# An encoder layer's attention: the product with v in two matmuls instead of three, the denominator on VectorE, the remainders on GpSimd

## The chip, the cores and the metric

The kernel runs on one NeuronCore of a Trainium2 chip. The metric is the time on the device of one launch, in microseconds (us). The launch holds six stages that run one after the other on the same core.

## The reference

One transformer layer on 1024 prompt tokens and 2048 sample tokens, each group with 16 learned meta tokens in front of it. Eight heads of grouped-query attention (GQA, 64 wide, two key/value heads) and eight heads of latent attention (MLA, query and key 96 wide, value 64 wide), an output projection, a mixture of experts and a last norm:

```python
s = einsum('bqhgd,bkhd->bhgqk', q, k) * scale      # per head; q of the group against its keys
p = softmax(s, axis=-1)                            # over the group's keys and the 16 meta keys
o = einsum('bhgqk,bkhe->bqhge', p, v)
h += W_out[ norm(GQA(u)) | norm(MLA(u)) ],  u = RMSNorm(h)
h += HierMoE(RMSNorm(h));  out = RMSNorm(h)[:, 16:]
```

Everything is float32. The kernel multiplies in `float32r`, a rounded form; a factor that has to be exact is split into a rounded part (`hi`) and a remainder (`lo`), and the products of the parts are added up in PSUM.

## The kernel before, in words

**Stages.** `stage_project` makes q, k and v of all heads and stores their hi and lo parts in DRAM; `stage_attend` computes attention; then come the output projection, the routing, the experts and the last norm. The change touches the first two.

**Attention's items.** A head's work is a fixed list of 86 items. An item is 128 keys (a chunk) against 512 queries (a block). There are six blocks, four of the sample (16 chunks and the 16 meta keys: 17 items each) and two of the prompt (8 chunks and the meta keys: 9 items each); a block's meta item is its last. So a head has 80 full items and 6 meta items. Every engine walks the same list in its own program, with semaphores between them.

**One item.** TensorE (`qk`, line 1064) makes the scores transposed, keys by queries, in one of two banks `psS`: two matmuls for a GQA head, three for an MLA head. The row maximum has been put in as one more row of the product, so that ScalarE (`exp`, line 936) can read the bank twice with Exp, once into the rounded `p_hi` and once into the exact `prob`. VectorE (`remainder`, line 981) subtracts them into `p_lo`; for eight of the items GpSimd does so (line 929). Then TensorE (`pv`, line 1075) adds v_hi p_hi + v_lo p_hi + v_hi p_lo into a bank `psO`, three matmuls of 512 columns, two items behind `qk`. v has a column of ones as its 65th, so that the bank's 65th row is the denominator. `p_hi`, `p_lo` and `prob` have four slots. GpSimd makes v_hi and v_lo of the next head itself (`split`, line 897).

**The maxima of the next head.** In the same slots each engine also does a piece of the next head's row maxima: TensorE a matmul of 128 queries by 512 keys into one of two banks `psM` (`unit`, line 1098), VectorE a maximum over it (line 996). There are 80 such units, laid over 72 of the slots; 24 small matmuls into `psK` do the meta keys (line 1105). `finish` joins the maxima, `row` turns them and sends them through DRAM into a row of q.

**The end of a block.** ScalarE copies `psO` to `oT` (`o_out`), TensorE turns it with four transposes (`o_turn`, line 1117), VectorE multiplies by the reciprocal of the denominator (`normalise`, line 1015), and the result is stored.

**Projection.** For each pair of token tiles `mla` (line 626) makes eight units in two banks `psX`; the two `v` units are copied out by ScalarE alone (line 416), the `k` and `n` units by ScalarE and VectorE. A bank is free for the unit after next when its last reader has gone over it. GpSimd copies the GQA heads' v (line 330).

## Time and profile before

| | us |
|---|---|
| three runs: lowest, median, highest | 4121.14, 4127.71, 4137.02 |
| the profiled execution, its own time | 4129.44 |
| its span, first to last instruction | 4127.6 |
| granted TensorE clock, mean over the span | 0.952 of full speed |

Busy shares over the span are TensorE 91%, VectorE 67%, ScalarE 58%, GpSimd 13%. They are means over six stages with different limits, so they say little of one stage. "Busy" of a matmul counts from its start to a modelled end, and successive ones overlap; the same holds to a lesser degree of VectorE and ScalarE. What an instruction costs in a full queue is the distance from its start to the next one's start, here called its pitch.

### The profile page before, as it was taken

How to read it: one execution, taken by the hardware profiler on the slowest of the kernel's cores; microseconds unless marked ns; L12 is line 12 of the kernel's file. 1: busy time of each engine (PE TensorE's matmuls, PEld its weight loads, DVE VectorE, ACT ScalarE, POOL GpSimd, SP SyncE). 2: the span in 40 equal slices, each digit the busy share in tenths (PEclk: the TensorE clock that was granted, in tenths of full speed). 3: DMA queues.
4: the chain of work that ended last, by engine and by line, in shares of the span. 5: the costliest groups of instructions: out<-in, count | busy, mean ns of one | idle time of the engine just before them, and what ended most of it. 6: DMA issues, size and time to landing. Idle time of an engine off the chain costs nothing. (4 is left out here: it accounts for less than half of the span.)

```text
span 4127.6 us, 59990 instructions
## 1 busy us (share of the span) xinstructions
PE 3739.1 (91%) x16747; PEld 2729.3 (66%) x16748; DVE 2763.0 (67%) x4425; ACT 2377.5 (58%) x4123; POOL 554.9 (13%) x553
## 2 busy tenths in 40 slices
PE   7999948999999999999999999996999569999992
PEld 7888825666666666667667666764777456666661
DVE  5656547878878898878677777854343556666564
ACT  4443304777777777766676666676333135555554
POOL 0000000111111111110110111100000013333331
PEclk9999967999999999999999999998999889999996
DMA  4464570220222112221121122002333158888787
GB/s 164 153 218 160 189 187 16 61 54 20 56 62 61 44 33 52 61 61 26 41 60 42 25 61 49 16 7 90 137 129 135 53 169 240 239 244 251 230 239 270
DMA packets 308135, 454.66 MB, mean 110 GB/s; under 512 B 118230, under 2 KB 245490, under 8 KB 296850
## 3 DMA queue, kind: packets, MB, share of 16 engines
q1 hardware_dynamic: 241942, 359.85, 29.1%
q0 software_dynamic: 18576, 67.64, 6.9%
q10 hardware_dynamic: 47376, 24.26, 2.0%
q8 instruction: 115, 1.88, 0.2%
q14 instruction: 126, 1.03, 0.1%
HBM read 305.68 MB, written 146.05 MB: 109 GB/s over the span
## 5 line engine op out<-in xcount | busy, mean ns | idle before, releaser
L940 ACT ACTIVATE b_p_hi<-b_psS 128x512 fp32r<-128x512 f32 (+1 forms) x1376 | 822.0, 597 | 587.6 <-PE b_psS L1071 575.8
L1071 PE MATMUL b_psS<-b_q,b_k 96*128 96x512 f32 (+3 forms) x3440 | 1051.3, 403 | 24.7 <-issue 18.2
L988 DVE TENSOR_TENSOR b_p_lo<-b_prob,b_p_hi 128x512 fp32r<-128x512 f32 x1152 | 830.1, 722 | 252.3 <-ACT b_prob L943 207.1
L943 ACT ACTIVATE b_prob<-b_psS 128x512 f32<-128x512 f32 (+1 forms) x1376 | 815.0, 592 | 1.1
L1071 PEld LDWEIGHTS b_psS<-b_q,b_k 96*128 96x128 f32 (+3 forms) x3440 | 628.0, 186 | 255.9 <-issue 25.6
L996 DVE TENSOR_REDUCE b_mx_s<-b_psM 128x1 f32<-128x512 f32 x1024 | 691.5, 687 | 86.6 <-PE b_psM L1102 66.6
L1102 PE MATMUL b_psM<-b_k,b_q 128*128 128x512 f32 (+1 forms) x1280 | 516.1, 424 | 54.2 <-DMA b_v<-V 39.4
L1094 PE MATMUL b_psO<-b_p_hi,b_v_hi 128*65 128x512 f32 x1280 | 516.2, 403 | 26.3 <-DVE b_p_lo L988 24.4
L1094 PE MATMUL b_psO<-b_p_hi,b_v_lo 128*65 128x512 f32 x1280 | 509.5, 398 | 0.0
L1094 PE MATMUL b_psO<-b_p_lo,b_v_hi 128*65 128x512 f32 x1280 | 509.0, 398 | 0.0
L929 POOL TENSOR_TENSOR b_p_lo<-b_prob,b_p_hi 128x512 fp32r<-128x512 f32 x128 | 166.6, 1301 | 1684.8 <-ACT b_prob L943 1684.8
L1102 PEld LDWEIGHTS b_psM<-b_k,b_q 128*128 128x128 f32 (+1 forms) x1280 | 251.7, 197 | 157.5 <-DVE b_mx_s L996 52.4
L1094 PEld LDWEIGHTS b_psO<-b_p_lo,b_v_hi 128*65 128x65 f32 x1280 | 175.9, 137 | 125.3 <-issue 5.1
L1094 PEld LDWEIGHTS b_psO<-b_p_hi,b_v_hi 128*65 128x65 f32 x1280 | 176.6, 138 | 118.9 <-DVE b_p_lo L988 51.3
L1094 PEld LDWEIGHTS b_psO<-b_p_hi,b_v_lo 128*65 128x65 f32 x1280 | 177.2, 138 | 110.1 <-issue 4.0
L2051 PE MATMUL e_psG<-e_w_gu,e_xT 128*128 x512 | 233.2, 598 | 11.0 <-SPq L1874 10.0
L612 PE MATMUL a_psZ<-a_w_hi,a_xT_hi 128*128 128x396 f32 x600 | 209.4, 349 | 24.6 <-DVE a_w_lo L569 24.6
L612 PE MATMUL a_psZ<-a_w_hi,a_xT_lo 128*128 128x396 f32 x600 | 207.3, 345 | 0.0
L612 PE MATMUL a_psZ<-a_w_lo,a_xT_hi 128*128 128x396 f32 x600 | 206.5, 344 | 0.0
L996 DVE TENSOR_REDUCE b_mx_p<-b_psM 128x1 f32<-128x512 f32 x256 | 173.9, 687 | 30.7 <-PE b_psM L1102 27.6
L1934 ACT ACTIVATE e_wg_hi<-e_w_gu 128x2048 fp32r x64 | 122.7, 1917 | 106.5 <-SPq L1874 85.2
L2000 DVE TENSOR_TENSOR e_wd_lo<-e_w_dn,e_wd_hi 128x2048 fp32r<-128x2048 f32 x64 | 146.7, 2292 | 37.6 <-ACT e_wd_hi L1948 35.8
(247 smaller groups left out, 5274.9 us busy)
## 6 DMA issues: line engine op xcount, KB each, us to landing
e_w_gu<-w_gate SPq DMA_DIRECT2D x32, 1024.0 KB, 7.7
e_w_gu<-w_up SPq DMA_DIRECT2D x32, 1024.0 KB, 10.0
e_w_dn<-w_down SPq DMA_DIRECT2D x32, 1024.0 KB, 13.6
a_x_raw<-xallT SPq DMA_DIRECT2D x25, 512.0 KB, 5.0
a_x<-xall SPq DMA_DIRECT2D x25, 512.0 KB, 4.2
c_o<-O SPq DMA_DIRECT2D x24, 512.0 KB, 4.8
c_x<-xall SPq DMA_DIRECT2D x24, 512.0 KB, 3.6
H<-c_h SPq DMA_DIRECT2D x24, 512.0 KB, 2.7
```

What stands on the lines that cost most here:

```text
L612: i = nc.tensor.matmul(psZ[:, b, 0:ZW], xx[:, s, c, :], ww[:, c, b * ZW:b * ZW + ZW], start=n == 0, stop=n == 3 * KC - 1)
L929: nc.gpsimd.tensor_tensor(p_lo[:, slot, :], prob[0:kn, slot, :], p_hi[0:kn, slot, :].bitcast(F32), ALU.subtract).then_inc(lo_ready_pool, 1)
L940: nc.scalar.activation(p_hi[0:kn, (s * NI + j) % NP, :], psS[0:kn, j % 2, :], ACT.Exp)
L943: nc.scalar.activation(prob[0:kn, (s * NI + j) % NP, :], psS[0:kn, j % 2, :], ACT.Exp).then_inc(p_ready, 1)
L988: nc.vector.tensor_tensor(out, prob[0:kn, slot, :], p_hi[0:kn, slot, :].bitcast(F32), ALU.subtract).then_inc(lo_ready, 1)
L996: nc.vector.tensor_reduce(dst, psM[:, u % 2, :], AX.X, ALU.max).then_inc(m_free, 1)
L1071: m = nc.tensor.matmul(psS[0:kn, j % 2, :], kk[s][0:r, k], qq[s][0:r, q], start=n == 0, stop=n == len(passes) - 1)
L1094: m = nc.tensor.matmul(psO[0:VC, b % 2, :], vv[s][:, vc, :], pp[:, slot, :], start=first and n == 0, stop=last and n == 2)
L1102: nc.tensor.matmul(psM[:, u % 2, :], q0[s][0:r, q * P:q * P + P], k0[s][0:r, kc:kc + 512], start=True, stop=True).then_inc(m_psum, 1)
L1934: nc.scalar.activation(wg_hi[:, :, :], w_gu[:, bass.ds(w * KC, HK), :], ACT.Copy).then_inc(wg_rounded, 1)
L2000: nc.vector.tensor_tensor(wd_lo[:, c, :], w_dn[:, bass.ds(w * HC, HC), :], wd_hi[:, c, :].bitcast(F32), ALU.subtract).then_inc(wd_ready, 1)
L2051: nc.tensor.matmul(psG[:, s, :], xT[:, c - HK, :], w_gu[:, bass.ds(w * KC + c, 1), :].rearrange("p o n -> p (o n)"), start=c == HK, stop=F ...
```

## The change

**v side by side.** v's hi and lo parts are made in the projection stage and stored next to each other, 128 columns for each head (`VC = 2 * VD`), and loaded as one stationary tile. One matmul with `p_hi` and one with `p_lo` (`pv_hi`, `pv_lo`) then give hi and lo sums in the two halves of `psO`'s 128 rows. The column of ones is gone. The two halves are added at the end of the block: for GQA heads by a matmul with a doubled identity (`pair_id`) in place of the transpose, for MLA heads by transposes back into `psO` and an add on VectorE.

**The denominator.** VectorE adds every `prob` tile to an accumulator in a PSUM bank, `acc`, three items late (`den_add`), the last one of a block into `accS` in SBUF. `o_turn` sums it over the partitions: a one-column matmul for GQA, a transpose and a VectorE sum for MLA.

**The remainders.** GpSimd makes `p_lo` of all 80 full items. VectorE makes the remainder of meta items only.

**Meta keys.** They are the second item of each block rather than the last, and are stored both ahead of and behind the other keys. The maxima's units take them in: five units of 412 or 414 columns for a sample tile and three of 346 or 348 for a prompt tile, 104 units over 68 slots. The 24 small matmuls go.

**Depths.** Six slots instead of four; `pv_hi` two items behind `qk`, `pv_lo` four; `o_out`, `o_turn`, `normalise` and the store one or two items later.

```diff
-VC = VD + 1
+VC = 2 * VD
@@ projection, GpSimd v_copy
                 for copy in range(2):
-                    i = nc.gpsimd.tensor_copy(vst_g[:, b, j, copy:PAIRS:2, 0:VD],
-                                              z[:, s, ZV:ZCQ].rearrange("p (h c) -> p h c", c=VD))
+                    nc.gpsimd.tensor_copy(vst_g[:, b, j, copy:PAIRS:2, 0:VD].bitcast(F32R), src)
+                pool.drain()
+                for copy in range(2):
+                    i = nc.gpsimd.tensor_tensor(vst_g[:, b, j, copy:PAIRS:2, VD:VC].bitcast(F32R), src,
+                                                vst_g[:, b, j, copy:PAIRS:2, 0:VD], ALU.subtract)
@@ projection, VectorE mla_out
-                    if kind == "k":
+                    if kind == "v":
+                        r = META if B is None else P
+                        i = nc.vector.tensor_tensor(vst_m[0:r, j, :, VD:VC].bitcast(F32R),
+                                                    psX[0:r, u % 2, :].rearrange("p (h c) -> p h c", c=VD),
+                                                    vst_m[0:r, j, :, 0:VD], ALU.subtract)
+                    elif kind == "k":
@@ attention, items and units
-        R = 4
-        SPAN = 72
+        R = 6
+        HI_LAG, LO_LAG, DEN_LAG = 2, 4, 3
+        SPAN = 68
@@ attention, GpSimd
+                slot = slot_of(s, j)
+                pool.wait_ge(p_ready, h * NI + j + 3)
+                nc.gpsimd.tensor_tensor(p_lo[:, slot, :], prob[:, slot, :], p_hi[:, slot, :].bitcast(F32),
+                                        ALU.subtract).then_inc(lo_ready, 1)
@@ attention, ScalarE exp
-                act.wait_ge(pv_done, h * NI + j + 1)
+                act.wait_ge(pv_done, h * NI + j + 1 + NP - reuse(s, j))
+                act.wait_ge(den_done, h * NI + j + 1 + NP - reuse(s, j))
@@ attention, VectorE
+            def den_add(h, s, j):
+                _, _, kn, _, first, last = ITEMS[j]
+                slot = slot_of(s, j)
+                dve.wait_ge(p_ready, h * NI + j + 3)
+                if kn == META:
+                    nc.vector.tensor_tensor(p_hi[M_LO, slot, :], prob[0:kn, slot, :], p_hi[0:kn, slot, :].bitcast(F32),
+                                            ALU.subtract).then_inc(meta_lo_ready, 1)
+                dve.wait_ge(den_done, h * NI + j + NP)
+                if first:
+                    m = nc.vector.tensor_copy(acc[:, :], prob[:, slot, :])
+                else:
+                    out = accS[:, BLOCK_OF[j] % 2, :] if last else acc[0:kn, :]
+                    m = nc.vector.tensor_tensor(out, acc[0:kn, :], prob[0:kn, slot, :], ALU.add)
+                m.then_inc(den_done, 1)
@@ normalise, MLA heads
+                nc.vector.tensor_reduce(den[:, :], psT[:, :].rearrange("p (j c) -> p j c", c=P), AX.X, ALU.add)
+                dve.drain()
+                nc.vector.reciprocal(rden[:, :], den[:, :])
+                dve.drain().then_inc(t_free, 1)
+                dve.wait_ge(o_stored[b % 2], stored)
+                nc.vector.tensor_tensor(o_lo[:, :, :], tv[:, :, VD:2 * VD], rr, ALU.mult)
+                nc.vector.tensor_tensor(ost[:, b % 2, :, :], tv[:, :, 0:VD], rr, ALU.mult)
+                dve.drain()
+                nc.vector.tensor_tensor(ost[:, b % 2, :, :], ost[:, b % 2, :, :], o_lo[:, :, :], ALU.add).then_inc(o_ready, 1)
@@ attention, TensorE
-                for n, (vv, pp) in enumerate(((v_hi, p_hi), (v_lo, p_hi), (v_hi, p_lo))):
-                    m = nc.tensor.matmul(psO[0:VC, b % 2, :], vv[s][:, vc, :], pp[:, slot, :],
-                                         start=first and n == 0, stop=last and n == 2)
+                nc.tensor.matmul(psO[:, b % 2, :], v[s][:, vc, :], p_hi[:, slot_of(s, j), :], start=first, stop=False)
...
+                pe.wait_ge(lo_ready, h * (NI - NB) + j - metas + 1)
+                nc.tensor.matmul(psO[:, b % 2, :], v[s][:, vc, :], p_lo[:, slot_of(s, j), :],
+                                 start=False, stop=last).then_inc(pv_done, 1)
@@ o_turn
+                    if gqa:
+                        nc.tensor.matmul(psT[:, c * VD:c * VD + VD], oT[:, b % 2, cc], pair_id[:, :], start=True, stop=True)
+                        m = nc.tensor.matmul(psT[:, SUP * VD + c:SUP * VD + c + 1], accS[:, b % 2, cc], ones[:, :],
+                                             start=True, stop=True)
+                        continue
+                    nc.tensor.transpose(psO[:, b % 2, cc], oT[:, b % 2, cc], ident[:, :])
+                    m = nc.tensor.transpose(psT[:, cc], accS[:, b % 2, cc], ident[:, :])
```

## Rows read from the trace of the kernel before

**Rows 1.** Page, first part: TensorE's busy time of the whole span.
```profile
PE 3739.1 (91%) x16747; PEld 2729.3 (66%) x16748; DVE 2763.0 (67%) x4425; ACT 2377.5 (58%) x4123; POOL 554.9 (13%) x553
```

**Rows 2.** Windows view: length, engines' busy us, clock; ahead of attention, and attention.
```profile
0.00:664.00 664.00, 553.56 (x2672) 481.07 (x2673) 377.21 (x937) 221.31 (x390) 27.82 (x69) 0.90 0.54 167
664.00:2838.00 2174.00, 2118.16 (x9331) 1460.43 (x9331) 1701.85 (x2715) 1582.03 (x2943) 267.86 (x226) 0.98 0.20 43
```

**Rows 3.** Windows view over seven GQA heads, then over six MLA heads.
```profile
777.31:1680.80 903.49, 871.82 (x3831) 589.28 (x3830) 753.04 (x1226) 690.44 (x1288) 124.25 (x105) 0.98 0.23 50
1821.19:2700.50 879.31, 860.76 (x3798) 606.18 (x3797) 674.65 (x1051) 596.40 (x1104) 105.34 (x90) 0.98 0.19 41
```

**Rows 4.** Timeline, VectorE: joining of the maxima, once a head; start, duration.
```profile
777.31 0.18 DVE L1006 TENSOR_TENSOR b_nmx<-b_nmx,b_nmx_m 128x24 f32<-128x24 f32 x1
...
1680.80 0.18 DVE L1006 TENSOR_TENSOR b_nmx<-b_nmx,b_nmx_m 128x24 f32<-128x24 f32 x1
```

**Rows 5.** Page, groups: busy us, mean ns of one | idle before, its releaser.
```profile
L996 DVE TENSOR_REDUCE b_mx_s<-b_psM 128x1 f32<-128x512 f32 x1024 | 691.5, 687 | 86.6 <-PE b_psM L1102 66.6
```

**Rows 6.** Timeline, TensorE, inside an MLA item: start, duration.
```profile
2300.69 0.39 PE L1102 MATMUL b_psM<-b_k,b_q 96*128 96x512 f32 x1
2300.91 0.39 PE L1094 MATMUL b_psO<-b_p_hi,b_v_hi 128*65 128x512 f32 x1
2301.14 0.39 PE L1094 MATMUL b_psO<-b_p_hi,b_v_lo 128*65 128x512 f32 x1
```

**Rows 7.** Timeline, TensorE: the 24 small matmuls of a head.
```profile
773.70 2.74 PE L1108 MATMUL b_psK<-b_k,b_q 128*128 128x16 f32 x24
```

**Rows 8.** Timeline, VectorE with a full queue.
```profile
827.82 0.68 DVE L988 TENSOR_TENSOR b_p_lo<-b_prob,b_p_hi 128x512 fp32r<-128x512 f32 x1
828.42 1.28 DVE L996 TENSOR_REDUCE b_mx_s<-b_psM 128x1 f32<-128x512 f32 x2
```

**Rows 9.** Tile view: the maximum over 384 columns; min/median/max ns.
```profile
L1001 DVE TENSOR_REDUCE b_nmx_m<-b_psK x16: 557/558/558, 655.1 to 2699.7; 128x24 f32<-128x384 f32 x16
```

**Rows 10.** Timeline, VectorE: a block's normalisation.
```profile
696.40 1.29 DVE L996 TENSOR_REDUCE b_mx_s<-b_psM 128x1 f32<-128x512 f32 x2
697.87 0.18 DVE L1019 RECIPROCAL b_rden<-b_psT 128x4 f32<-128x4 f32 x1 [0.18 <-issue]
698.23 0.42 DVE L1022 TENSOR_TENSOR b_ost<-b_psT,b_rden 128x256 f32<-128x256 f32 x1 [0.18 <-issue]
698.88 0.69 DVE L988 TENSOR_TENSOR b_p_lo<-b_prob,b_p_hi 128x512 fp32r<-128x512 f32 x1 [0.22 <-ACT b_prob L943]
```

**Rows 11.** Timeline: GpSimd and VectorE at the same time, VectorE reading SBUF twice.
```profile
786.54 2.46 POOL L916 TENSOR_TENSOR b_v_lo<-b_v,b_v_hi 128x1040 fp32r<-128x1040 f32 x1
...
786.64 3.51 DVE L988 TENSOR_TENSOR b_p_lo<-b_prob,b_p_hi 128x512 fp32r<-128x512 f32 x2 [0.21 <-issue]
```

**Rows 12.** The same with one of VectorE's inputs in PSUM.
```profile
746.75 1.30 POOL L929 TENSOR_TENSOR b_p_lo<-b_prob,b_p_hi 128x512 fp32r<-128x512 f32 x1 [10.11 <-ACT b_prob L943]
...
747.02 0.42 DVE L1022 TENSOR_TENSOR b_ost<-b_psT,b_rden 128x256 f32<-128x256 f32 x1 [0.16 <-issue]
```

**Rows 13.** Tile views: GpSimd's remainder, and a subtraction out of PSUM.
```profile
L929 POOL TENSOR_TENSOR b_p_lo<-b_prob,b_p_hi x128: 1270/1291/1567, 700.4 to 2827.4; 128x512 fp32r<-128x512 f32 x128
...
L541 DVE TENSOR_TENSOR a_stage<-a_psX,a_stage x26: 191/691/693, 70.4 to 540.7; 128x512 fp32r<-128x512 f32 x24, 128x32 fp32r<-128x32 f32 x2
```

**Rows 14.** Timeline, projection: the v units of one batch on TensorE and ScalarE.
```profile
181.72 1.88 PE L644 MATMUL a_psX<-a_w_vup,a_ckvT 128*128 128x512 f32 x4
184.86 1.99 PE L651 MATMUL a_psX<-a_ckvT,a_w_kup 128*128 128x256 f32 x8 [1.26 <-ACT a_vst_m L416]
...
184.23 1.06 ACT L416 ACTIVATE a_vst_m<-a_psX 128x512 f32<-128x512 f32 x2
```

**Rows 15.** Timeline, TensorE: maxima of the first head, before attention starts.
```profile
604.49 1.41 PE L1102 MATMUL b_psM<-b_k,b_q 128*128 128x512 f32 x2 [0.17 <-DVE b_mx_s L996]
606.07 1.41 PE L1102 MATMUL b_psM<-b_k,b_q 128*128 128x512 f32 x2 [0.17 <-DVE b_mx_s L996]
```

359 lines of the change are left out of this document (172 added, 187 removed).

## The prediction

> **What bounds the kernel now.** I read the page's first part, then the windows by stage, then single heads, then timelines for the pitch of each kind of instruction. TensorE leads on the page [rows 1]; attention is 2174 of the 4127.6 us [rows 2]. The joining of the maxima comes once a head, so the distance between two of them is a head's time [rows 4]. The same marks frame the windows [rows 3]: seven GQA heads take 903.49 us, 129.1 each; six MLA heads take 879.31, 146.5 each. TensorE is idle for 32 and 19 us there, so both kinds go by TensorE, MLA heads nearly without a gap. Its matmuls of 512 columns start 0.23 us apart [rows 6], although each lasts 0.39 there. VectorE is busy for 107.6 us of a GQA head's 129.1, ScalarE for 98.6: whatever goes onto VectorE has little room.
>
> **TensorE after.** A full item loses one matmul of three with v: 80 a head, 80 x 0.23 = 18.4 us. The stationary tile grows from 65 to 128 columns at no cost, since `qk` has 128 and keeps the 0.23 pitch [rows 6]. The 24 small matmuls go, 2.7 us [rows 7]. The units stay at nearly the same columns in shorter pieces: 80 x 0.188 + 24 x 0.16 = 18.9 us (412 and 346 columns at full clock, 0.172 and 0.144, and the 0.016 by which 0.23 exceeds 512 columns), against 80 x 0.23 = 18.4. The turns grow. For a 128-column stationary tile the nearest pitch is 2.74/24 = 0.11 us [rows 7]. MLA has eight a block, 0.9 us; GQA four matmuls with `pair_id` and four with `ones`, in float32, each listed as two instructions as L644 is (four rows for two units [rows 14]): 16 x 0.11 = 1.8 us. Sum for MLA: 86 x 3 + 80 x 2 + 6 = 424 matmuls x 0.23 = 97.5, units 18.9, turns 5.4: 122 us. GQA: 338 x 0.23 = 77.7, units 18.9, turns 10.7: 107 us.
>
> **VectorE after.** A 512-element instruction has a pitch of 0.60 us in a full queue, whether a subtraction or a maximum [rows 8]. Maxima: 687 ns at 512 columns [rows 5], 558 at 384 [rows 9], so 1.0 ns an element; 412 columns pitch at 0.50, 346 at 0.43, and the head's 104 take 40 + 10.4 = 50.4 us (80 x 0.60 = 48 before). Adds: 86 x 0.60 = 51.6, where 78 subtractions stood. Whether an add that also writes PSUM costs the same no row shows. From below it can't be under 0.60, the rate of any 512 elements; from above, a dependent instruction after a drain starts 0.18 after the end of the one before [rows 10], 0.69 + 0.18 = 0.87. I take 0.60: a subtraction that reads PSUM lasts 691 ns [rows 13], the SBUF one 0.68 or 0.69 [rows 8], and a maximum usually stands between two adds, which hides the wait on `den_done`. The Trainium skill ("VectorE: DVE Perf Modes", section "The TRN2 errata") gives a PSUM source 62 cycles more than an SBUF source; by it the 86 adds would cost 5.6 us a head more, 90 us in all. The trace disagrees: 691 ns out of PSUM against 0.68 to 0.69 us out of SBUF is no difference.
>
> A block's normalisation puts about 1.2 us between two other instructions [rows 10], from 696.40 + 2 x 0.60 to 698.88. GQA keeps it. MLA adds a 512-element sum (0.6), one more multiply and an add of 256 (0.35 each) and two drains (0.2 each): 2.9 us.
>
> **GpSimd after.** It takes 80 remainders of 1.29 us [rows 13]. What separates two in a row no row shows; between the shortest, 1.27, and the longest, 1.57, I take 1.3, which is 104 us a head. `split` goes. Beside it VectorE: a subtraction with both inputs in SBUF stood still until GpSimd's was over, 3.51 us for two [rows 11]. With one input in PSUM it kept its 0.42 us inside GpSimd's 1.30 [rows 12]. `den_add` reads PSUM and SBUF, so I cost no collision for it. The Trainium skill ("SBUF — State Buffer", section "SBUF: two separate sides") has this as an exclusive lock that a VectorE instruction takes if it has two SBUF inputs or runs in a two-port mode; by that rule, the trace agrees. Two-SBUF instructions are left: the meta remainder, and the MLA heads' last add. Each waits for a running 1.29, half of it on average, 0.65 us. The stall behind L916, 3.51 - 0.60 - 0.69 = 2.2 us a head, goes.
>
> **A head.** In the 68 slots with units GQA has on VectorE: adds 40.8, maxima 50.4, four meta remainders 2.4 and their waits 2.6, three normalisations 3.6: 99.8 us, against TensorE's 88 (268 matmuls, the units, four turns) and 64 x 1.3 = 83 of GpSimd. VectorE ends last. In the other 18 slots GpSimd does, 16 x 1.3 = 20.8 (ScalarE's 98.6/86 is at most 1.15 an item). Together 120.6; I add 2.9 for the clock, granted at 0.98 [rows 3], and for trading places: 123.5. MLA, VectorE: 40.8 + 50.4 + 2.4 + 2.6 + 3 x 2.9 + 3 x 0.65 = 106.9, TensorE 100. Other slots: 18 adds one after another at 0.75, 13.5, meta 1.2, three normalisations 8.7, the joining and row 1.5: 24.9. Together 131.8, with 4.2 for bursts of VectorE that hold up a TensorE only 7 us ahead: 136.
>
> **Elsewhere.** Projection: a v bank is now freed by VectorE after ScalarE, 0.69 later [rows 13], and TensorE already waits 1.26 there [rows 14]; 12 batches x 0.8 = 10 us. At the other end it may be nothing, if TensorE makes it up; twice that if VectorE comes late. GpSimd's two more small subtractions a tile hide in a tile's time, some 20 us (L541's first to last, 470 us, for 24 tiles [rows 13]). V grows from 65 to 128 columns a head. Mid-stage that hides; at the change of stages the last store (256 tokens x 8 heads x 63 x 4 bytes, 0.5 MB) and the first head's sample load (0.5 MB) take 3 us each at 167 GB/s [rows 2] if nothing covers them; I take 4 (0 to 8). The first head's maxima run ahead of everything at 1.58 us for two [rows 15]; 100 columns fewer save 0.10 on each engine at 1.0 ns a column, 166 fewer 0.17, so two take 1.39 and 1.25, and all 104 take 70.6 us instead of 63.2, less 0.6 for L1001: +7. Eight extra stores of meta columns, once, hide in SP's queue.
>
> **Sum** against the execution's own 4129.4 us: GQA 8 x (129.1 - 123.5) = 45; MLA 8 x (146.5 - 136) = 84; costs 10 + 4 + 7 = 21. 4129.4 - 45 - 84 + 21 = 4021. The median of the runs is 1.7 lower: **4020 us**, 2.6% faster. The 80 x 16 matmuls alone are worth 294 us; over half is lost to VectorE.
>
> **Rivals.**
> TensorE stays the bound: the added depth evens VectorE out, and nobody meets the lock. GQA 118 (VectorE's sum without waits), MLA 122 plus 3 for the clock, 125: 8 x 11.1 + 8 x 21.5 - 21 = 240, 3890 us. For it: six slots. Against it: `psM` still has two banks, so TensorE can run at most two units ahead.
> GpSimd becomes the bound: remainders at 1.57 us, the longest seen [rows 13], 80 of them 126 us. GQA 130, MLA 138: 4129 + 7 - 68 + 21 = 4090 us. For it: meta and add instructions hold the lock against it too. Against it: the median is 1.29.
> Slower than before: the accumulator in PSUM serialises VectorE. Every add costs 0.87 instead of 0.60, 86 x 0.27 = 23 us more in heads in which VectorE ends last. 4021 + 16 x 23 = 4389 us. With a price of only 0.065 it would be 4021 + 89 = 4110, no change. It passes the time before once an add costs 109/(16 x 86) = 0.08 us more than I took. For it: each add waits on the one before, and no row shows such a write. Against it: [rows 12, 13].
> The change does not do its part only if the two matmuls pitched like three; `qk` rules that out.
>
> **How the numbers follow.** My forecast 0.53 (3970 to 4070), TensorE 0.20, GpSimd 0.13, the add at 4110 0.03, at 4389 0.11. A measurement of this kernel tells no change from a difference of 0.5%, 21 us. Faster by more: 0.53 + 0.20 + 0.10 of GpSimd's case = 0.83; within: its other 0.03 and the add's 0.03, 0.06; slower: 0.11. The range reaches from just above TensorE's case over GpSimd's to the add at 4110: 3900 to 4120. It leaves out the dear add and the lower end of TensorE's case, some 0.2.
>
> **What would show it.** The joinings 121 to 126 us apart in GQA heads and 133 to 140 in MLA heads; VectorE's idle time small in both; `den_add` at 0.69 us listed and 0.60 pitch beside GpSimd instructions of 1.29; TensorE waiting on VectorE at `psM`; k units of the projection waiting 2 us. A `den_add` above 0.75, or GpSimd above 1.4, would make the forecast wrong upwards; GQA heads under 118, downwards.

## The result, and the profile after

Four runs of the changed kernel took 4303.23 to 4317.05 us, median 4312.33; four of the kernel before 4121.14 to 4137.02, median 4125.83. The ratio is 1.0439, with a 95% interval from 1.0416 to 1.0461. The forecast was 4020 us, 2.6% faster; the kernel became 4.4% slower, and the time lies outside the range.

The windows view (length, busy us of TensorE, its weight loads, VectorE, ScalarE, GpSimd, granted clock, DMA share, GB/s) of the changed kernel, by stage, answers to [rows 2]:

```profile
0.00:684.00 684.00, 556.69 (x2675) 483.04 (x2677) 402.05 (x987) 222.17 (x391) 39.85 (x105) 0.89 0.57 178
684.00:3018.00 2334.00, 2135.84 (x8818) 1624.00 (x8816) 1916.70 (x3414) 1519.88 (x2844) 1659.71 (x1280) 0.91 0.20 45
3018.00:4309.80 1291.80, 1067.73 (x4744) 786.98 (x4744) 682.73 (x771) 574.18 (x792) 249.21 (x258) 0.93 0.62 193
```

The windows are cut at round times. By the trace's own marks, the first Exp of attention and the next stage's first load, attention starts 19 us later (21 were forecast) and takes 155 us more, where it was to become 129 us shorter. The stages behind it, which the change does not touch, take 1295 us (1287 before; 1287 to 1299 in the experiments below). The same view over seven GQA heads and six MLA heads, between the same marks as [rows 3]:

```profile
803.60:1813.03 1009.43, 936.78 (x3779) 690.29 (x3779) 817.82 (x1479) 663.13 (x1246) 727.37 (x560) 0.89 0.23 51
1957.88:2876.19 918.31, 822.36 (x3464) 646.20 (x3463) 765.17 (x1375) 573.26 (x1068) 622.62 (x481) 0.93 0.21 47
```

A GQA head takes 144.2 us instead of 129.1, an MLA head 153.1 instead of 146.5. TensorE has fewer matmuls, yet is busy longer in GQA heads (936.78 against 871.82): the granted clock fell from 0.98 to 0.89, and in MLA heads to 0.93. The clock knows two levels, 2.4 and 1.2 GHz, so 0.89 means that 32.1 us of each GQA head ran at half clock (5.4 before), and 0.93 means 22.2 us of each MLA head (5.9 before).

The sizes of single instructions are those forecast. From the page's groups (busy us, mean ns of one | idle before, releasers) and the listing of VectorE's meta remainder in GQA heads (min/median/max ns):

```profile
L931 POOL TENSOR_TENSOR b_p_lo<-b_prob,b_p_hi 128x512 fp32r<-128x512 f32 x1280 | 1660.8, 1311 | 833.1 <-ACT b_prob L951 817.4
L1002 DVE TENSOR_TENSOR b_acc<-b_acc,b_prob 128x512 f32<-128x512 f32 (+1 forms) x1184 | 817.1, 690 | 64.1 <-issue 37.9
L1010 DVE TENSOR_REDUCE b_mx_s<-b_psM 128x1 f32<-128x412 f32 (+1 forms) x1280 | 706.1, 578 | 180.1 <-PE b_psM L1130 168.1
...
L995 DVE TENSOR_TENSOR b_p_hi<-b_prob,b_p_hi x42: 681/1534/1825, 813.9 to 1807.8; 16x512 fp32r<-16x512 f32 x42
```

An add in PSUM lasts 690 ns and has the pitch of 0.60 us. The meta remainder, 0.68 us by itself, lasts 1.53 in the median and 1.39 in the mean: it waits for a running GpSimd instruction, 0.71 us on average instead of the 0.65 forecast.

What was not forecast is what happens where VectorE's work comes in one piece. VectorE and then TensorE at the end of a GQA block (start, duration; in brackets idle time before, and what ended it):

```profile
739.75 0.57 DVE L1010 TENSOR_REDUCE b_mx_s<-b_psM 128x1 f32<-128x412 f32 x1
740.36 1.52 DVE L995 TENSOR_TENSOR b_p_hi<-b_prob,b_p_hi 16x512 fp32r<-16x512 f32 x1
741.81 0.68 DVE L1002 TENSOR_TENSOR b_acc<-b_acc,b_prob 16x512 f32<-16x512 f32 x1
742.52 1.08 DVE L1010 TENSOR_REDUCE b_mx_s<-b_psM 128x1 f32<-128x412 f32 x2
...
740.91 0.64 PE L1099 MATMUL b_psS<-b_q,b_k 128*128 128x512 f32 x2
743.16 0.46 PE L1130 MATMUL b_psM<-b_k,b_q 128*128 128x414 f32 x1 [1.61 <-DVE b_mx_s L1010]
743.46 0.40 PE L1111 MATMUL b_psO<-b_p_hi,b_v 128*128 128x512 f32 x1
743.79 0.49 PE L1118 MATMUL b_psO<-b_p_hi,b_v_meta 48*128 48x512 f32 x1
744.21 0.52 PE L1145 MATMUL b_psT<-b_pair_id,b_oT 128*128 128x64 f32 x2
744.52 0.53 PE L1146 MATMUL b_psT<-b_ones,b_accS 128*128 128x1 f32 x2
```

For 2.2 us VectorE reads no bank of `psM`. TensorE has filled both and stands still for 1.61 us. At 744.4, 1.3 us behind the stop and just as the block's turn with its 64- and 1-column matmuls has begun, the clock falls to half. The windows view of the next 6.8 us, and TensorE in them:

```profile
744.50:751.30 6.80, 6.80 (x26) 6.19 (x26) 2.58 (x6) 1.28 (x3) 1.27 (x1) 0.50 0.00 0
...
748.48 0.55 PE L1130 MATMUL b_psM<-b_k,b_q 128*128 128x412 f32 x1
748.82 0.63 PE L1111 MATMUL b_psO<-b_p_hi,b_v 128*128 128x512 f32 x1
749.25 0.55 PE L1130 MATMUL b_psM<-b_k,b_q 128*128 128x412 f32 x1
```

512 columns now take 0.43 us and not 0.23, TensorE is busy all the time, and VectorE only 2.58 of 6.80 us: for that long TensorE is the bound. In MLA heads the piece is the normalisation:

```profile
2356.19 1.08 DVE L1010 TENSOR_REDUCE b_mx_s<-b_psM 128x1 f32<-128x412 f32 x2 [0.92 <-PE b_psM L1130]
2357.44 0.69 DVE L1039 TENSOR_REDUCE b_den<-b_psT 128x4 f32<-128x512 f32 x1 [0.17 <-issue]
...
2359.33 0.90 DVE L1047 TENSOR_TENSOR b_ost<-b_ost,b_o_lo 128x256 f32<-128x256 f32 x1
...
2361.38 0.46 PE L1130 MATMUL b_psM<-b_k,b_q 96*128 96x414 f32 x1 [2.35 <-DVE b_mx_s L1010]
```

A third place is the start of a head. The row of maxima goes to DRAM and back by the sync engine's queue. Its issues around one MLA head's start, then TensorE's first matmul of that head:

```profile
1953.44 0.51 SPq L857 DMA_DIRECT2D b_q<-QNH  x1
...
1958.45 0.40 SPq L857 DMA_DIRECT2D b_v<-V  x1
1963.54 7.84 SPq L891 DMA_DIRECT2D MX<-b_nmxT  x1
1975.07 0.23 SPq L894 DMA_DIRECT2D b_q<-MX  x1
...
1977.22 1.64 PE L1099 MATMUL b_psS<-b_q,b_k 97*128 97x512 f32 x3 [4.28 <-DMA b_q<-MX]
```

The store comes 5 us behind nine large loads and its issue takes 7.84 us (4.5 in the median of the 16 heads); before the change it came 13 us behind them and took 0.3. TensorE's waits by releaser (total us, times, longest), in the six MLA heads of the kernel before and then of the changed one:

```profile
PE b_psO L1094 <- DVE b_p_lo L988: 8.7, 6, 1.5
PE b_psS L1071 <- issue: 6.6, 2, 3.5
PE b_psM L1102 <- DVE b_mx_s L996: 3.3, 2, 2.1
```

```profile
PE b_psM L1130 <- DVE b_mx_s L1010: 43.5, 36, 2.4
PE b_psS L1099 <- DMA b_q<-MX: 26.8, 6, 5.8
PE b_psM L1130 <- DVE b_mx_p L1010: 15.2, 12, 2.3
```

### The profile page after: what moved, and what is told of

The parts are those of the page before. It is cut to its first block and busy times, and to the rows that moved or that the text cites. A ratio compares the mean times of both kernels' runs of the same rounds, so it can differ in the third digit from the quotient of the medians.

```text
span 4309.8 us, 62526 instructions
## 1 busy us (share of the span) xinstructions
PE 3760.3 (87%) x16235; PEld 2894.0 (67%) x16236; DVE 3001.5 (70%) x5171; ACT 2316.2 (54%) x4027; POOL 1948.8 (45%) x1642
## 5 line engine op out<-in xcount | busy, mean ns | idle before, releaser
L931 POOL TENSOR_TENSOR b_p_lo<-b_prob,b_p_hi 128x512 fp32r<-128x512 f32 x1280 | 1660.8, 1311 | 833.1 <-ACT b_prob L951 817.4
L1002 DVE TENSOR_TENSOR b_acc<-b_acc,b_prob 128x512 f32<-128x512 f32 (+1 forms) x1184 | 817.1, 690 | 64.1 <-issue 37.9
L1010 DVE TENSOR_REDUCE b_mx_s<-b_psM 128x1 f32<-128x412 f32 (+1 forms) x1280 | 706.1, 578 | 180.1 <-PE b_psM L1130 168.1
L1130 PE MATMUL b_psM<-b_k,b_q 128*128 128x412 f32 (+7 forms) x1664 | 669.9, 409 | 184.7 <-DVE b_mx_s L1010 102.9
L1111 PE MATMUL b_psO<-b_p_hi,b_v 128*128 128x512 f32 x1280 | 537.6, 420 | 0.2 <-ACT b_prob L951 0.2
L1123 PE MATMUL b_psO<-b_p_lo,b_v 128*128 128x512 f32 x1280 | 531.9, 416 | 0.7 <-POOL b_p_lo L931 0.7
L1111 PEld LDWEIGHTS b_psO<-b_p_hi,b_v 128*128 128x128 f32 x1280 | 261.6, 204 | 57.0 <-issue 2.2
L1123 PEld LDWEIGHTS b_psO<-b_p_lo,b_v 128*128 128x128 f32 x1280 | 260.3, 203 | 35.9 <-POOL b_p_lo L931 1.2
L1010 DVE TENSOR_REDUCE b_mx_p<-b_psM 128x1 f32<-128x346 f32 (+1 forms) x384 | 185.7, 510 | 20.0 <-PE b_psM L1130 19.1
L2088 PEld LDWEIGHTS e_psG<-e_w_gu,e_xT 128*128 128x128 f32 x512 | 98.1, 192 | 118.0 <-issue 113.3
```

The costliest lines, as they stand in the source:

```text
L931: nc.gpsimd.tensor_tensor(p_lo[:, slot, :], prob[:, slot, :], p_hi[:, slot, :].bitcast(F32), ALU.subtract).then_inc(lo_ready, 1)
L1002: m = nc.vector.tensor_tensor(out, acc[0:kn, :], prob[0:kn, slot, :], ALU.add)
L1010: nc.vector.tensor_reduce(dst, psM[:, u % 2, 0:n_keys], AX.X, ALU.max).then_inc(m_free, 1)
L1111: nc.tensor.matmul(psO[:, b % 2, :], v[s][:, vc, :], p_hi[:, slot_of(s, j), :], start=first, stop=False)
L1123: nc.tensor.matmul(psO[:, b % 2, :], v[s][:, vc, :], p_lo[:, slot_of(s, j), :], start=False, stop=last).then_inc(pv_done, 1)
L1130: nc.tensor.matmul(psM[:, u % 2, 0:kn], q0[s][0:r, q * P:q * P + P], k0[s][0:r, kc:kc + kn], start=True, stop=True).then_inc(m_psum, 1)
```

## The experiments

Theory A: TensorE stops where VectorE's work comes in one piece at a block's end and where the row is late, and the clock falls behind such stops; stops and half clock together are the loss. Theory B: VectorE's sum is the bound, the clock costs nothing. Theory C: the clock falls because TensorE has less to do throughout. "Half" is the time at half clock, "stops" TensorE's idle stretches above 0.6 us, both in us per head, from each profiled execution.

A fall is a drop of the granted clock from full to half. In the changed kernel's six MLA heads all 26 falls began inside a stop or within 1.7 us behind one. In its seven GQA heads 7 of the 33 falls began behind a stop and ahead of the turn, 5 at a turn with no stop before it, and 21 when a stop and the first matmuls of the turn both lay in the 3.1 us before, so that there the two causes cannot be told apart. Over the windows of all 18 profiled executions of the table (stops that began at half clock, 61, left out), none of the 204 stops of 0.6 to 1.5 us was followed by a fall within 4 us, 254 of the 309 of 1.5 to 2.5 us were, and 188 of the 191 longer ones; MLA heads by themselves give 0 of 133, 150 of 200 and 92 of 93.

The kernel before was run again beside each group of experiments, with medians 8 us apart, so small differences between groups are better read from the ratios. x1, x3 and x4 rest on two runs each.

| kernel | median us | ratio to before (95%) | GQA head, half, stops | MLA head, half, stops |
|---|---|---|---|---|
| before | 4126 to 4134 | 1 | 129.1, 5.4, 3.5 | 146.5, 5.8, 3.1 |
| after | 4312.33 | 1.0439 (1.0416 to 1.0461) | 144.2, 32.1, 8.9 | 153.1, 22.2, 15.2 |
| x1_fill | 4432.74 | 1.0737 (1.0687 to 1.0787) | 146.3, 14.1, 5.7 | 168.3, 21.0, 13.4 |
| x2_noden | 4133.62 | 1.0008 (0.9993 to 1.0024) | 127.7, 13.7, 6.0 | 146.1, 15.9, 12.8 |
| x3_metapool | 4220.29 | 1.0222 (1.0173 to 1.0271) | 134.9, 17.1, 7.7 | 150.7, 20.5, 15.5 |
| x4_spread | 4203.59 | 1.0182 (1.0136 to 1.0228) | 135.5, 18.0, 5.4 | 147.3, 15.9, 13.1 |
| x5_row | 4353.42 | 1.0537 (1.0519 to 1.0554) | 150.6, 41.3, 13.8 | 150.3, 17.6, 15.5 |
| x6_all3 | 4167.04 | 1.0090 (1.0073 to 1.0106) | 133.9, 16.6, 8.6 | 143.3, 13.7, 12.5 |
| x7_all3_turnfill | 4197.69 | 1.0167 (1.0148 to 1.0185) | 138.2, 10.7, 6.1 | 143.2, 13.1, 12.3 |
| x8_all3_split | 4155.99 | 1.0070 (1.0049 to 1.0092) | 133.8, 16.1, 8.6 | 142.3, 14.8, 11.5 |
| x9_rowact | 4276.54 | 1.0344 (1.0319 to 1.0369) | 144.5, 35.2, 8.7 | 147.9, 17.1, 11.7 |
| x10_best | 4103.56 | 0.9926 (0.9901 to 0.9952) | 129.7, 10.2, 4.0 | 139.2, 7.4, 8.9 |
| x11_best_late | 4167.26 | 1.0074 (1.0047 to 1.0100) | 132.5, 10.7, 6.0 | 145.6, 14.8, 12.5 |
| x12_best_pair | 4106.98 | 0.9924 (0.9894 to 0.9953) | 130.0, 10.7, 4.5 | 138.8, 12.5, 1.6 |
| x13_inter | 4096.92 | 0.9921 (0.9902 to 0.9940) | 128.2, 7.3, 3.8 | 139.6, 9.1, 8.6 |
| x14_inter_pair | 4072.17 | 0.9860 (0.9840 to 0.9879) | 128.4, 6.8, 4.2 | 135.4, 5.1, 1.5 |
| x15_late8 | 4117.54 | 0.9970 (0.9958 to 0.9982) | 132.5, 12.7, 4.3 | 139.6, 9.7, 8.4 |
| x16_early | 4103.26 | 0.9939 (0.9925 to 0.9952) | 130.4, 10.7, 5.5 | 138.9, 9.1, 3.7 |

**x1_fill.** Each matmul of the maxima is issued twice.

```diff
+                nc.tensor.matmul(psM[:, u % 2, 0:kn], q0[s][0:r, q * P:q * P + P], k0[s][0:r, kc:kc + kn],
+                                 start=True, stop=True)
                 nc.tensor.matmul(psM[:, u % 2, 0:kn], ...
                                  start=True, stop=True).then_inc(m_psum, 1)
```

> Every maxima matmul of the changed kernel is issued twice into the same bank, which changes no result: 104 x 0.16 to 0.19 = 19 us more TensorE work a head, evenly spread. Theory A (TensorE stops at block ends because VectorE's work comes in one piece there, and these stops take the clock to half): the stops stay, the extra work delays VectorE little; time 4300 to 4400, clock in attention up by 0.01 to 0.03 from 0.91. Theory B (VectorE's sum is the bound and the clock costs nothing): within 1% of 4312. Theory C (the clock falls because TensorE's stream is thinner all along): clock back to 0.97, time 4200 to 4260.

Half clock in GQA heads went from 32.1 to 14.1 us and stops from 8.9 to 5.7, but the head took 2.1 us more. The 104 extra matmuls cost 18.9 us by the forecast's own price; 9 of it is the half clock's gain, and most of the rest went into time in which TensorE had waited. So the clock does matter (B alone falls), but this filler did not pay for itself, and the time is above what each theory gave. That more work brought the clock back in GQA heads is also what C says. In MLA heads, where TensorE had little slack, the filler cost 15.2 and the half clock stayed, since the stops did; by C it should have gone.

**x2_noden.** All but the first copy and the last add of a block are left out.

```diff
+                if not first and not last:
+                    dve.sem_inc(den_done, 1)
+                    return
```

> Of the denominator's adds only the first copy and the last add of a block are made; the rest is left out, so outputs are wrong by the denominator. VectorE loses 74 adds of 0.60 us a head, 44 us. Theory A: stops mostly go, clock back to 0.96 or more, GQA heads near 118 us, MLA near 130, time about 4129 - 8 x 11 - 8 x 16 + 21 = 3935. Theory B: the same time, by VectorE's sum alone, 3900 to 3950, clock no matter. Theory C: TensorE's stream is as thin as in the changed kernel, so the clock stays near 0.91 and the time stays above 4050.

179 us less, so much of the loss hangs on VectorE's load, but 4134 is 200 above A and B. VectorE is busy for 72.1 us of a GQA head's 127.7 here: it can't be the bound by its sum. C's time fits (above 4050), but not its clock, which is 0.95 in both windows and not 0.91. 12.8 us of stops are left in an MLA head, at the two places that do not depend on the adds:

```profile
PE b_psM L1133 <- DVE b_mx_s L1013: 30.2, 18, 1.8
PE b_psS L1102 <- DMA b_q<-MX: 28.9, 6, 5.8
```

**x3_metapool.** GpSimd makes the meta item's remainder too, so that no VectorE instruction of a GQA head waits for GpSimd's hold on SBUF.

```diff
+                if ITEMS[j][2] == META:
+                    pool.wait_ge(lo_ready, h * (NI - NB) + j - BLOCK_OF[j])
+                    nc.gpsimd.tensor_tensor(p_hi[M_LO, slot, :], prob[0:META, slot, :], p_hi[0:META, slot, :].bitcast(F32),
+                                            ALU.subtract).then_inc(meta_lo_ready, 1)
+                    return
...
-                if kn == META:
-                    nc.vector.tensor_tensor(p_hi[M_LO, slot, :], prob[0:kn, slot, :], ...
```

> The meta remainder is made by GpSimd, so VectorE has no instruction with two SBUF inputs left in GQA heads. Theory A: the 0.6 us and the 0.8 us wait for GpSimd's lock go from every block end, stops shrink from 1.65 to under 0.5 us in GQA heads, the clock there recovers to 0.94 or more, GQA heads 144 to 132, MLA 153 to 150; time about 4190. Theory B: 6 x 1.4 = 8 us a head less in GQA, 4 in MLA, 4215. Theory C: as B for the stop, clock unchanged, 4250 to 4280.

92 us less for 96 instructions moved, whose whole time on VectorE was 116 us with their waits. The gain is mostly in GQA heads, 9.3 us each (2.4 in MLA heads); half of the half clock went. By its time alone, 4220, this is B's forecast (4215) rather than A's (4190); the clock in GQA heads, 0.94, is what A said. The stops at `psM` became shorter but did not fall under 0.5 us: 11 of 1.0 to 1.5 us stood there, and no fall of the clock followed one of them. With `psM` out of the way TensorE now waited for the late row in GQA heads too, 25.9 us in seven, against 1.8 in the changed kernel.

**x4_spread.** The same 104 units, but none in the seventh slot behind a block's last item, where VectorE normalises, and about half as many in the two before it.

```diff
+        SHARE = [0.0 if j - 7 in END_OF else 0.55 if j - 5 in END_OF or j - 6 in END_OF else 1.0
+                 for j in range(R, R + SPAN)]
         for u in range(NU):
-            UNIT_AT.setdefault(R + u * SPAN // NU, []).append(u)
+            at, k = (u + 0.5) / NU * sum(SHARE), 0
+            while sum(SHARE[:k + 1]) <= at:
+                k += 1
+            UNIT_AT.setdefault(R + k, []).append(u)
```

> The same 104 maxima units, but one instead of one or two in the slots five and six behind a block's end and none in the seventh, where VectorE normalises. No work is added or removed. Theory A: the stops at psM shrink, the clock recovers by 0.02 to 0.04, time 4200 to 4260. Theory B: the same sum on VectorE, 4300 to 4320. Theory C: no change of clock, within 0.5% of 4312.

No engine has less to do, and the time falls by 109 us, 8.7 us per GQA head and 5.8 per MLA head. Half clock in GQA heads fell from 32.1 to 18.0 us with TensorE's work unchanged, where C forecast no change. This is the plainest proof that no engine's sum set the time.

**x5_row.** The sync engine sends the maxima's row ahead of the next sample load.

```diff
+                row(h + 1, 1 - s, nxt)
                 if more:
                     sp.wait_ge(pv_done, h * NI + SAMPLE_LAST + 1 + NP)
                     load(h + 2, i + 1, s, kind, "s")
-                row(h + 1, 1 - s, nxt)
```

> The sync engine issues the next head's maxima row (store to DRAM, load back) ahead of the sample load of the head after, nothing else changed. Theory A (part of it): the row came late because its store was queued right behind 8 to 10 large sample loads (issue of store to issue of load 6 to 13 us after, 2 to 4.6 before). Then the stop at a head's start goes: 4.4 to 5.8 us for each of 7 MLA starts, 2 to 3 for each GQA start, with the half-clock stretch behind it (MLA 22 us of half clock a head to about 15), 4312 - 7 x 5 - 8 x 2.5 - 7 x 3 = about 4235. Theory C (the stop at a head's start is hidden time, VectorE's sum decides): within 10 us of 4312. Rival: the large loads are then late in turn and the time stays; the stop would move from the row to the load.

41 us slower, where A gave 77 less: the rival. The wait on the row went, and this came in its place, with half clock behind it (MLA heads):

```profile
PE b_psM L1130 <- DMA b_v<-V: 36.6, 6, 9.8
```

**x6_all3** is x3, x4 and x5 in one.

> Three edits in one: the meta item's remainder on GpSimd (alone -92 us), fewer maxima units in the two slots behind a block's end and none in the third (alone -109), the row ahead of the sample load. If each removes a stop of its own, the gains add: 4312 - 92 - 109 - 60 = about 4050, half clock under 10 us per GQA head. If the first two remove the same stop (the lump of VectorE's work at a block's end), the result is 4312 - 110 - 60 = about 4140 and half clock stays at 15 to 18 us per GQA head. I expect between them, 4100.

4167, and again a wait for v's load of up to 8.6 us, 5.3 us a head (36.5 and 32.1 us in the two windows). 4100 was expected. The three edits' own differences, -92, -109 and +41, would give 4152: x3 and x4 nearly add up, x5's edit is the wrong mend.

**x7_all3_turnfill.** As x6, with a wide matmul behind each of three pairs of a GQA turn.

```diff
+                        if c < SUP - 1:
+                            nc.tensor.matmul(psT[:, 260:512], ident[:, :], oT[:, b % 2, 0:252], start=True, stop=True)
```

> As the kernel with three edits, with one more matmul of 252 columns (exact float32, its output unused) behind each of the first three pairs of a GQA turn. It tests what takes the clock to half right behind a GQA turn. If it is the turn's narrow matmuls (64 columns and 1 column), the dips that begin 0 to 1.5 us behind a GQA turn (some 18 of 23 in seven heads) go and half clock falls below 5 us per GQA head; the fillers themselves cost 18 x 0.42 = 7.6 us per GQA head, so the time is about equal to slightly above the kernel without them. If it is a stop that precedes, the dips stay and the time is 50 to 60 us above. MLA heads: no change.

In x6 nine of twelve falls of the clock in seven GQA heads began 0.2 to 1.7 us behind the end of a turn, with no stop before it; here none of seven did, and all seven stand at long stops. Half clock fell from 16.6 to 10.7 us, not below 5 as expected, and the time rose by 31, as the fillers cost. MLA heads are unchanged. So a stretch of 1- and 64-column matmuls can take the clock down with no stop, though it does not always: 9 of x6's 42 turns had a fall behind them.

**x8_all3_split.** As x6; the last multiply and add of an MLA normalisation come one slot later.

```diff
+                    if j - 8 in END_OF:
+                        normalise_2(h, END_OF[j - 8], gqa)
```

> As the kernel with three edits, with the second half of an MLA head's normalisation (one multiply, one add, 0.9 + 0.4 us) moved one slot later. Theory A: the stop of 1.7 to 2.3 us at an MLA block's end comes from VectorE's work in one piece; cut in two, with psM's two banks between, it falls by 1.0 to 1.3 us, six times a head: 147 to about 141 per MLA head, 8 x 6 = 48 us less. If VectorE's sum decides, nothing (within 10 us). GQA heads: no change.

1.0 us per MLA head, not 6; the two medians differ by 11 us and their ranges overlap. That VectorE's wait for the turn, in the half that was not moved, makes the stop instead is what x11 and x15 try.

**x9_rowact.** The changed kernel, the row's two DMAs on ScalarE's queue three and six slots behind its making.

```diff
+                    if not last and j == ROW_AT + 3:
+                        row_store(act, h + 1)
+                    if not last and j == ROW_AT + 6:
+                        row_load(act, h + 1, 1 - s, nxt)
```

> The next head's maxima row goes through DRAM by two DMAs of ScalarE's queue, three and six slots behind the row's making, instead of the sync engine's queue behind the sample load; that load stays where it was. Theory A: the stop at a head's start (MLA 4.4 to 5.8 us, GQA 2 to 3) goes and, unlike with the row issued ahead of the load on the sync engine, no load comes late in its place: 4312 - 6 x 5 - 8 x 2.5 - the half clock behind them (some 6 us less at half clock per head, each worth 0.5 us, 14 x 3 = 42) = about 4220. Rival: the stop is only hidden time of VectorE's sum, within 15 us of 4312.

5.1 us less per MLA head, nothing in GQA heads: 36 us, where 92 were expected. In the changed kernel the late row was a cost of MLA heads alone; its GQA heads had waited for it for only 1.8 us in seven, so there was no stop to remove.

**x10_best** is x3, x4 and x9 in one.

> Meta remainder on GpSimd, units kept away from the slots behind a block's end, and the row by ScalarE's queue. The kernel with the row ahead of the load on the sync engine took 4167 and showed a wait of 6 us a head for v's load (half of it is the row's move). Without that wait 6 us for each of 14 heads go and half clock falls to some 10 us per head: 4167 - 14 x 6 + 0 = about 4085 (range 4060 to 4120), faster than before (4129). If VectorE's sum (123 us busy per GQA head, 137 per MLA head) is the bound now, it stays at 4140 or above.

4103.56, within the expected range and 0.7% faster than the kernel before. Alone the three gave 92, 109 and 36, together 209 of these 237 us. The 123 and 137 us of VectorE in the text above add up listed durations, which overlap; by the windows view it is busy for 108.0 and 123.2 us of a head. GQA and MLA heads of x10:

```profile
793.41:1701.20 907.79, 873.01 (x3775) 624.73 (x3775) 756.26 (x1436) 659.52 (x1246) 763.79 (x603) 0.96 0.25 57
1836.39:2671.41 835.02, 781.21 (x3464) 620.12 (x3463) 739.16 (x1339) 571.34 (x1068) 664.50 (x517) 0.97 0.23 52
```

**x11_best_late** moves x10's normalisation and store one slot later.

```diff
-                    if j - 7 in END_OF:
+                    if j - 8 in END_OF:
                         normalise(...)
...
-                    if j - 9 in END_OF:
+                    if j - 10 in END_OF:
                         o_store(...)
```

> As the last, with each block's normalisation (and its store) one slot later. VectorE waits 1.3 us at each of the 6 ends of an MLA block for TensorE's turn (48 us in six heads), and TensorE then stops 1.5 us for psM. Theory A: one slot later the turn is done, VectorE does not wait, TensorE's stop falls by about 1.3 us a block, 6 x 1.3 = 8 us per MLA head and half as much per GQA head: some 60 to 90 us less. If VectorE's wait is only slack, the time is within 10 us of the last.

64 us slower, where 60 to 90 less were expected. The normalisation now stood in a slot with units again.

**x12_best_pair** gives x10's MLA heads the GQA heads' turn (a 64-column matmul with `pair_id` and a 1-column sum for each 128 queries), so VectorE's 2.7 us at a block's end become 0.6.

```diff
-                    if gqa:
+                    if True:
                         nc.tensor.matmul(psT[:, c * VD:c * VD + VD], oT[:, b % 2, cc], pair_id[:, :], start=True, stop=True)
```

> As the kernel with the three edits, with the MLA heads' turn made as the GQA heads' (matmul with the doubled identity, one-column denominator sum): VectorE's work at an MLA block's end is a reciprocal and one multiply (0.6 us) instead of 2.7 us and 1.3 of waiting. Theory A (VectorE's lump stops TensorE): 2.1 us less a block, 12 us per MLA head, up to 90 us in all, the stops on psM nearly gone. Rival: the narrow columns of this turn take the clock to half behind each turn as in GQA heads (0.4 to 1.5 us behind it, 3.4 us each), which gives back 6 x 3.4 / 2 = 10 us per head: no gain. GQA heads: no change.

The stops went, 8.9 to 1.6 us a head, and the time did not move. One turn of it on TensorE and what follows:

```profile
2145.79 0.43 PE L1162 MATMUL b_psT<-b_pair_id,b_oT 128*128 128x64 f32 x2
...
2147.40 0.33 PE L1163 MATMUL b_psT<-b_ones,b_accS 128*128 128x1 f32 x2
2147.59 1.15 PE L1116 MATMUL b_psS<-b_q,b_k 97*128 97x512 f32 x3
2148.55 0.55 PE L1147 MATMUL b_psM<-b_k,b_q 96*128 96x414 f32 x1
2148.89 0.63 PE L1128 MATMUL b_psO<-b_p_hi,b_v 128*128 128x512 f32 x1
```

A turn takes 1.80 us instead of 0.9, 5.4 more a head, and half clock rose by 5.1 us, worth 2.6: together 8.0, against the 7.3 that the stops gave back. The matmul at 2148.89 is at half clock, with no stop before it. Nine of the eleven falls between 1860 and 2300 us began within 1.0 us of a turn's end, and 15 of the 36 turns in the six heads had a fall in them or within 2 us behind.

**x13_inter**: the turn's four pairs laid one by one between wide matmuls of two slots, on top of x15. **x14_inter_pair**: the same with x12's turn. **x15_late8**: x11 with the slot without units moved along.

```diff
                     qk(h, s, gqa, j)
+                    turn(7, 1)
...
                     pv_hi(h, s, j - HI_LAG)
+                    turn(7, 2)
...
                     pv_lo(h, s, j - LO_LAG)
-                    if j - 6 in END_OF:
-                        o_turn(h, END_OF[j - 6], use(h, END_OF[j - 6], last), gqa)
+                    turn(6, 0)
+                    turn(7, 3)
```

```diff
-        SHARE = [0.0 if j - 7 in END_OF else 0.55 if j - 5 in END_OF or j - 6 in END_OF else 1.0
+        SHARE = [0.0 if j - 8 in END_OF else 0.55 if j - 6 in END_OF or j - 7 in END_OF else 1.0
```

> Meta remainder on GpSimd, row by ScalarE's queue, normalisation and store one slot later with the slot without units moved along (as the kernel late8), and the turn's four pairs of matmuls laid one by one between wide matmuls of two slots instead of in one stretch. Theory: the GQA turn's narrow stretch takes the clock to half 0 to 1.5 us behind it; broken up it does not. Half clock per GQA head from 10 to 5 us or less, so 129.7 to 127; MLA as late8. Total 20 us below late8, about 4050. Rival (the dips come from the switch itself, or from the stops): half clock and time as late8 within 8 us.

> As the last, with the MLA heads' turn of the GQA kind. x12 had no stops in MLA heads (1.6 us per head) but 12.5 us of half clock and 5.4 us more of turning, 138.8 per head. Theory (narrow stretch): half clock falls to 4 us, so 138.8 - 4 = 135 per MLA head, and 127 per GQA head: 4107 - 8 x 4 - 8 x 3 = about 4050. Rival: half clock stays at 12 us per MLA head, 4100.

> The three edits, with normalisation and store one slot later and the slot without units moved one later too. If x11 (4167) was slower only because VectorE had units and normalisation in the same slot again, this is faster than x10 (4104): VectorE no longer waits 1.3 us for the turn, TensorE's stop in MLA heads falls from 8.9 us a head to about 3: 4104 - 8 x 6 = about 4055. If a later normalisation is bad by itself, it stays at 4120 or above.

Breaking up the turn took half clock in GQA heads from 12.7 to 7.3 us and the head from 132.5 to 128.2 (x15 to x13), and in MLA heads with narrow turns from 12.5 to 5.1 and from 138.8 to 135.4 (x12 to x14, which also takes in x15's edits; these had not helped MLA heads). Turns with a fall in them or within 2 us behind went from 10 to 4 of 42, and from 15 to 4 of 36. The profiled executions of x15 and x13 were each the slowest of their kernel, 12 and 15 us above its median; the medians differ by 21 us, 2.6 per GQA head rather than 4.3. MLA heads of x13 keep their transposes and did not gain. x13 and x14 were expected at about 4050; x14, at 4072, is the fastest kernel, 1.4% faster than before. Its two windows:

```profile
794.45:1693.03 898.58, 862.59 (x3776) 617.15 (x3774) 756.38 (x1437) 660.64 (x1247) 763.34 (x603) 0.97 0.25 57
1829.08:2641.58 812.50, 801.43 (x3752) 653.47 (x3751) 661.00 (x1231) 572.30 (x1068) 660.10 (x517) 0.98 0.24 54
```

x15 recovered 50 of the 64 us that x11 had lost (43 by the ratios), so the slot explains most of it, but was not faster than x10 as expected (4117.54, its ten runs from 4104.70 to 4129.71). VectorE waited for the turn at 12 of 36 ends of MLA blocks instead of all 36 in x10, yet TensorE's stops stayed at 8.4 us a head (8.9), where 3 were expected: that wait is not what made them. x12, which shortens VectorE's own work there, removed them. That a later normalisation has a cost of its own is neither shown nor excluded.

**x16_early**: x14 with the row's DMAs at `ROW_AT + 2` and `ROW_AT + 4`.

> As x14 (4072), with the maxima row stored one slot earlier and loaded two slots earlier in ScalarE's queue. Theory: the 2.5 us wait at each GQA head's start goes, and the half-clock stretch that begins there (3.4 to 10 us a head): 8 x (2.5 + 2) = 36 less, about 4040. Rival: ScalarE now waits for the row's making and store and its Exp instructions come later: within 10 us of 4072.

31 us slower than x14: the rival's mechanism, at three times its price. The load now comes before the store is through, and ScalarE, which issues both, stands before its next Exp, 5 us a head. ScalarE's waits from 780 to 2680 us:

```profile
ACT b_p_hi L965 <- PE b_psS L1118: 468.8, 866, 7.8
ACT b_p_hi L965 <- DMA MX<-b_nmxT: 71.2, 14, 6.1
```

## Why the prediction was wrong

**The step that failed** is the last of "A head": from sums to time. It put a head at the sum of the engine that ends last in each stretch, and added "2.9 for the clock, granted at 0.98, and for trading places" in GQA heads and "4.2 for bursts of VectorE that hold up a TensorE only 7 us ahead" in MLA heads. Measured against the same sums (120.6 and 131.8) these terms are 23.6 and 21.3 us, 8 x 20.7 + 8 x 17.1 = 302 us too little, which is the whole miss and a little more (4312 - 4020 = 292).

**What stood in its place.** The forecast's 123.5 is VectorE's sum with little idle time. VectorE was busy for 116.8 us of a GQA head and idle for 27.4, of which 17.7 fell into stretches at half clock: in these 32.1 us it was busy for 14.3, while TensorE did half of its usual work. At full clock it was busy for 102.5 of 112.1 us, nearly as forecast. In an MLA head it was idle for 25.6 us, 10.3 of them at half clock.

TensorE's losses against the kernel before tell the same from the other side. Per GQA head, half clock went from 5.4 to 32.1 us, and a stretch at half clock does about half of its work, so 13.3 us; stops grew from 3.5 to 8.9, 5.4 us; a meta matmul of 48 rows and the one before it take 0.76 us where 0.46 was reckoned (last section), 1.8 us for six. Together 20.5, of 144.2 - 123.5 = 20.7 missing. Per MLA head: 8.2, 12.1 and 1.8, together 22.1, against 17.1 missing and the 4.2 already allowed for bursts. That these come so near is partly luck: a stop during which VectorE works stands in VectorE's sum already, so losses of TensorE can't simply be added to it. What is shown is the order: x4, which removes no work, gave back 8.7 us of a GQA head with 14.1 us less half clock and 3.5 less of stops. x10 needs 14.5 us less per GQA head and has 10.2 us at half clock, though only the 16-row remainders, 8.4 us with their waits, left VectorE. The row has a part in that: without x9's edit TensorE waited 3.7 us for it at each GQA head in x3 and x4, with it 2.5 in x10. That the clock's share is half of the time at half clock is arithmetic; x14 against x12 agrees (7.4 us less half clock, 3.4 less in the MLA head).

The Trainium skill has something on both sides of this. "TensorE: Matmul & The Clock Gate" in the Trainium skill, section "A second HAM failure mode: psum-queue depth-cycling", says of another kernel that cycling through PSUM banks lets the engine idle briefly between groups often enough for its clock to swing between the two levels. The trace agrees on the swinging, 33 falls in seven GQA heads against 9 before, though here they stand at single stops of 1.6 us and more and not at many short ones. The same page of the Trainium skill, section "Terms", puts the loss at the time at half clock times one half, which by the trace's 26.7 us more is the 13.3 us above.

**Assuming the clock stayed at 0.98** was the root. The forecast read 0.98 off a kernel whose TensorE hardly waited (4.5 us per GQA head), and carried it to one in which TensorE has 13 us of slack per GQA head and must wait somewhere. It waited in stops of 1.6 and 2.35 us, since `psM` has two banks and the bursts of VectorE are longer than two units; stops under 1.5 us had no fall behind them in the windows of any run. The new turn of the GQA heads, 64- and 1-column matmuls in place of transposes, is the other part of the mechanism; the forecast priced it by its time alone. How much of the changed kernel's 32.1 us belongs to which of the two is not shown.

**What held.** VectorE's own work: the forecast's terms for it over a whole GQA head (adds 51.6, maxima 50.4, meta remainders and their waits 7.5, normalisations 7.2) make 116.7 us, and it was busy for 116.8. The add in PSUM (0.69 listed, 0.60 pitch beside a maximum, no lock), GpSimd (1.31, forecast 1.29), the maxima (0.58) and the start of attention (19 us later, 21 forecast; TensorE's waits in the projection for `a_vst_m` grew from 15.4 to 25.0 us, forecast 10). The lock's wait of the meta remainder, 0.71 for 0.65 on average, was a small error in time but stood at the worst place.

**The rivals.** None was this. TensorE's case (3890) took the six slots for the depth that counts; the two banks of `psM` are. GpSimd's (4090) fell with 1.31 us. The dear add (4389) gave a time near the measured one by a mechanism that is absent. The sentence against the first rival, that TensorE can run at most two units ahead, was the right one, used only to refuse a better time.

**Not seen at all.** The row's trip. The change moved its making from slot 79 to 77 and `pv_done` two items later, so its store fell from 13 us behind the sample load to 5; that SP issues both stood in the kernel's code, and the forecast never asked what the moved row is queued behind. It cost 5.1 us per MLA head (x9), 36 us in all.

**Open.** Why half clock in GQA heads was 35.2 us in x9 and not 32.1 as before its edit. What holds x14's GQA heads: less the 5.1 us of idle TensorE and 3.4 for the clock, 119.9 of their 128.4 us are left, 13 more than the forecast's sum for TensorE, while VectorE is busy for only 108.1 and GpSimd for 109.0. Waits too short to show behind the modelled ends of matmuls may be in it; nothing was tried apart. A third bank for `psM` was not tried either, nor the changed kernel with the broken-up turn alone.

## What to carry to other kernels

If a change takes TensorE off the bound, ask where it will wait and for how long at once. Here stops of under 1.5 us had no fall of the clock behind them, those of 1.5 to 2.5 us mostly had one, and so had some stretches of 1- and 64-column matmuls; then the sum of work no longer tells the time. Look for the places where the engine that it waits for has work in one piece (here a block's end) and compare that piece with what the banks between them hold; thinning out other work around it was worth 109 us without removing any. Give a short round trip through DRAM a queue without large loads ahead of it, on an engine that can issue its second half when the first is already done.
